# Block inverses of the gated delta stage: the transposes of five levels moved from TensorE to VectorE

## What is computed

```python
gam = jnp.exp(jnp.where(incl, dec[..., :, None] - dec[..., None, :], -jnp.inf))
a_low = jnp.where(strict, jnp.einsum('bhnid,bhnjd->bhnij', kb, k) * gam, 0.0)
t_inv = lax.linalg.triangular_solve(a_low + eye, jnp.broadcast_to(eye, a_low.shape),
                                    left_side=True, lower=True, unit_diagonal=True)
u = t_inv @ vb
w = t_inv @ (kb * jnp.exp(dec)[..., None])
```

## Time and profile before

| what | us |
|---|---|
| median of 3 runs | 2214.6 |
| lowest and highest run | 2213.84, 2214.62 |
| span of the profiled execution | 2213.1 |
| median less that span | 1.5 |
| TensorE busy in the span | 2182.9 (99%) |
| VectorE busy | 1497.0 (68%) |
| GpSimd busy | 1060.0 (48%) |
| ScalarE busy | 919.4 (42%) |
| L1466 (transposes), 192 in all | 27.9 |
| L1368 (masking), 96 in all | 33.8 |
| L1385 (copy_predicated), 96 in all | 42.8 |

### The profile page before, as it was taken

One profiled execution on the slowest core, in us unless ns is written; L12 is line 12 of the kernel. 1 busy time (PEld: TensorE's weight loads), 2 busy tenths in 40 slices (PEclk: granted clock), 3 DMA queues, 4 the chain that ended last, 5 costly groups with the idle time before them and its releaser, 6 DMA issues.

```text
span 2213.1 us, 29764 instructions
## 1 busy us (share of the span) xinstructions
PE 2182.9 (99%) x10592; PEld 1829.7 (83%) x10592; DVE 1497.0 (68%) x3595; ACT 919.4 (42%) x1514; POOL 1060.0 (48%) x850
## 2 busy tenths in 40 slices
PE   8999999999999999999999999999999999999998
PEld 6888888999888888888888888888888888888886
DVE  4655698777643530478888888972359788787883
ACT  6555596444433332433333333333323333333343
POOL 3433203544343344266666666656247665555500
PEclk9999999999999999999999999999999999999999
DMA  4222255552143322234444444456479999999940
GB/s 177 79 94 77 90 187 177 193 186 92 46 148 111 114 114 76 77 129 143 157 148 146 149 143 143 143 186 213 160 261 398 378 383 346 357 346 363 359 165 39
DMA packets 168831, 403.34 MB, mean 182 GB/s; under 512 B 27648, under 2 KB 101632, under 8 KB 158368
## 3 DMA queue, kind: packets, MB, share of 16 engines
q1 hardware_dynamic: 133920, 334.77, 43.3%
q0 software_dynamic: 34816, 67.41, 8.3%
HBM read 336.84 MB, written 65.28 MB: 182 GB/s over the span
## 4 chain that ended last, share of the span: by engine, by line
PE 71%; DVE 1%; ACT 1%; issue 0%; DVEq 0%; SPq 0%
PE ps L1628 13%; PE ps L176 11%; PE ps L174 11%; PE ps L175 11%; PE ps L2713 8%; PE ps L2714 8%; PE ps L2712 8%; PE ps L1971 1%; DVE down_v_low_sb L2535 0%; ACT merge_high_sb L1584 0%; PE ps L1718 0%; ACT ffn_norm_scaled_sb L1859 0%; DVE h_sb L1677 0%; DVE down_w_ple_proj_low_sb L2581 0%; DVE merge_low_sb L1589 0%
## 5 line engine op out<-in xcount | busy, mean ns | idle before, releaser
L2219 POOL DMA_INDIRECT g_dense<-up_gates_summed_sb,up_gate_at_sb x384 | 421.9, 1099 | 253.4 <-issue 211.7
L174 PE MATMUL ps<-n_high_sb,up_u_high_sb 128*128 128x512 f32 x1024 | 398.5, 389 | 0.5 <-issue 0.5
L176 PE MATMUL ps<-n_high_sb,up_u_low_sb 128*128 128x512 f32 x1024 | 398.5, 389 | 0.1
L175 PE MATMUL ps<-n_low_sb,up_u_high_sb 128*128 128x512 f32 x1024 | 398.3, 389 | 0.0
L2712 PE MATMUL ps<-down_v_high_sb,down_w_high_sb 128*128 128x512 f32 x768 | 298.8, 389 | 0.0
L2714 PE MATMUL ps<-down_v_high_sb,down_w_low_sb 128*128 128x512 f32 x768 | 298.8, 389 | 0.0
L2713 PE MATMUL ps<-down_v_low_sb,down_w_high_sb 128*128 128x512 f32 x768 | 298.8, 389 | 0.0
L2628 ACT ACTIVATE down_v_high_sb<-down_v_sb 128x1024 fp32r<-128x1024 f32 x120 | 125.8, 1048 | 310.8 <-PE ps L2714 286.9
L2062 DVE TENSOR_TENSOR up_u_low_sb<-up_u_sb,up_u_high_sb 128x1024 fp32r<-128x1024 f32 x128 | 156.3, 1223 | 140.1 <-ACT up_u_high_sb L2238 123.5
L2250 ACT ACTIVATE up_gelu_sb<-ps 128x512 f32<-128x512 f32 x128 | 76.5, 598 | 387.7 <-PE ps L176 280.7
L2444 POOL DMA_INDIRECT expert_rows_sb<-expert_v,chosen_expert_sb x128 | 155.1, 1212 | 168.6 <-DVE h_sb L2494 69.6
(11 more groups left out here) (382 smaller groups left out, 4484.0 us busy)
## 6 DMA issues: line engine op xcount, KB each, us to landing
up_u_sb<-expert_u SPq DMA_DIRECT2D x128, 512.0 KB
down_v_sb<-expert_v SPq DMA_DIRECT2D x32, 2048.0 KB
a_dense<-up_gelu_sb SPq DMA_DIRECT2D x128, 256.0 KB
g_dense<-nought_sb SPq DMA_DIRECT2D x8, 3072.0 KB, 12.0
down_gelu_sb<-a_dense SPq DMA_DIRECT2D x32, 768.0 KB
down_gates_sb<-g_dense SPq DMA_DIRECT2D x32, 768.0 KB
w_slots_sb<-w_conv SPq DMA_DIRECT2D x19, 1024.0 KB, 4.8
gate_w_sb<-w_gates SPq DMA_DIRECT2D x16, 512.0 KB, 4.4
```

The source lines that it names most:

```text
L174: pe.matmul(out, ah, bh, start=k == 0, stop=False)
L175: pe.matmul(out, ah, bl, start=False, stop=False)
L176: last = pe.matmul(out, al, bh, start=False, stop=k == n - 1)
L2219: pool.indirect_dma_start(cells, at, summed[:, tt, k:k + 1], None).then_inc(stored[tt], 16)
```

## The change

In the five levels with b up to 32 an inverse still has nothing outside its diagonal 32 by 32 squares, so a transpose of each square in its place is the transpose of the whole. VectorE now makes it with one instruction a lane (`dve.transpose`, 128x256, SBUF to SBUF) from `invs[u]` to `first_part[u]`, and then masks `first_part[u]` in place. First all four lanes are transposed, then all four masked. TensorE transposes only in the last level (b = 64); its wait for `inv_done` of each lane stays in every level. The semaphore `turned` now counts once a trip, and a new one, `squares_turned`, orders VectorE's masking behind its own transposes.

```diff
     NL = len(LEVELS)
+    SQUARE = 32
+    TURNS = sum(b <= SQUARE for b in LEVELS)
...
     split_done = [m.sem(f"gdn_inv_split{u}") for u in U]
+    squares_turned = m.sem("gdn_inv_squares_turned")
...
             for lv in range(NL):
-                for u in U:
-                    dve.wait_ge(turned, by_lane(u, i * NL + (lv + 1)))
-                    dve.tensor_tensor(first_part[u][:, :, :], both(whole4(u)), pair(halves[:, lv, :]), ALU.mult).then_inc(first_done, 1)
+                if LEVELS[lv] <= SQUARE:
+                    for u in U:
+                        dve.wait_ge(inv_done, by_lane(u, i * (NL + 1) + (lv + 1)))
+                        dve.transpose(first_part[u][:, :, :].rearrange("p c n -> p (c n)"),
+                                      invs[u][:, :, :].rearrange("p c n -> p (c n)")).then_inc(squares_turned, 1)
+                    for u in U:
+                        dve.wait_ge(squares_turned, by_lane(u, i * TURNS + (lv + 1)))
+                        dve.tensor_tensor(first_part[u][:, :, :], first_part[u][:, :, :], pair(halves[:, lv, :]),
+                                          ALU.mult).then_inc(first_done, 1)
+                else:
+                    for u in U:
+                        dve.wait_ge(turned, by_lane(u, i + 1))
+                        dve.tensor_tensor(first_part[u][:, :, :], both(whole4(u)), pair(halves[:, lv, :]), ALU.mult).then_inc(first_done, 1)
...
                     pe.wait_ge(inv_done, by_lane(u, i * (NL + 1) + (lv + 1)))
-                    for c in range(TS):
-                        last = pe.transpose(whole4(u)[:, c, :], invs[u][:, c, :], sq(m, "eye"))
-                    last.then_inc(turned, 1)
+                    if LEVELS[lv] > SQUARE:
+                        for c in range(TS):
+                            last = pe.transpose(whole4(u)[:, c, :], invs[u][:, c, :], sq(m, "eye"))
+                        last.then_inc(turned, 1)
                 if lv == 4:
                     second_gate(0, 11)
```

## The result

| | before | after |
|---|---|---|
| median of runs, us | 2214.61 (4 runs, 2213.84 to 2215.30) | 2252.86 (4 runs, 2251.53 to 2253.94) |
| ratio, 95% interval | | 1.0174, 1.0160 to 1.0188 |
| profiled execution, us | 2214.62 | 2251.53 |
| its span; mean granted clock | 2213.1; 0.999 | 2250.0; 0.992 |
| first matmul behind the stage's barrier starts at | 595.96 | 633.68 |

The kernel is 38.3 us slower. The time is inside the range (2235 to 2260), but 8 us above what my forecast case allowed for itself (2238 to 2245).

The account below looks back on a forecast made before the run. The prediction took a closed 4.68 us loop through VectorE's queue and TensorE as the bound. Its terms, 20.0 + 5.8 - 0.7 = 25.1 us, added to 2214.6 gave 2239.7 us; stated range 2235 to 2260.

Parts of the forecast that it names:

- my forecast case: Whole kernel: VectorE's four added transposes lengthen the loop, 25.1 us slower, 2239.7 us, own range 2238 to 2245; chance 0.70.
- The bound: a closed loop of 2.15 + 2.53: One doubling level: copy_predicated to first product 2.15, then to next copy_predicated 2.53, 4.68 us; TensorE's transposes fill its gap.
- What the change removes ... Worth: nothing.: TensorE: removing 160 of 192 transposes, eight in each of 20 levels, gains nothing apart from the fifth level.
- rival (d): TensorE's clock falls to half because it idles, doubling 3.67 us of passes in 17 levels: 62 us more, 2302; chance 0.03.
- The transpose's interval, 0.36: VectorE between fourth copy_predicated and first masking: one transpose issues every 0.36 us, four make 1.44 us.
- Rival (a): VectorE's transpose is dearer, an interval up to 0.61: 40.8 us more, 2255; chance 0.10.
- The masking meets GpSimd: the first product 3.69 after the CP: First masking, both inputs in SBUF, contends with GpSimd's second_part; first product 3.69 us after first copy_predicated, in place of 2.15.
- 1.54 a level: Lengthening from first copy_predicated to first product in 13 levels (second to fourth, last trip's fifth): 20.0 us.
- rival (b): VectorE's transpose, too, waits for GpSimd: 2.98 a level, 45.9 us more, 2260; chance 0.08.
- The first level, 1.44 each: First level of four trips: TensorE waits for VectorE, so four transposes add 1.44 each, 5.8 us.
- The fifth level, -0.7: Fifth level, first three trips: gate matmuls cover VectorE and no longer follow lane 3's transposes, gaining some 0.23 each.
- The delay passes the barrier whole: Barrier at the stage's end: it released TensorE and no transfer crosses it, so the whole delay reaches what follows.

Follow-up runs that it names:

- e4: Kernel before without TensorE's transposes in the second to fifth level, nothing added on VectorE, results not the reference's; 2216.51 us, ratio 1.0012.
- e2: Changed kernel with TensorE making the eight transposes in every level again, unused in the first five levels; 2240.25 us, ratio 1.0119.
- e1: Changed kernel with four unused 128x256 matmuls a lane on TensorE in the five levels, except where gate matmuls follow; 2241.47 us, ratio 1.0129.
- e3: Kernel before with VectorE's four transposes added in five levels, their results overwritten by the masking, which still reads PSUM; 2237.27 us, ratio 1.0107.
- e5: Changed kernel with VectorE's transposes and maskings of the next level placed between this level's copy_predicated, second to fifth level; 2256.87 us, ratio 1.0197.
- e10b: Changed kernel, transposes and maskings interleaved between copy_predicated, with TensorE's transposes made in every level, unused in the first five; 2242.02 us, ratio 1.0118.
- e7: Kernel before with lane 3 alone transposed by VectorE in the second to fifth level, order else as before; 2220.54 us, ratio 1.0029.

## Why the prediction was right in direction and 13 us short

1. *The bound: a closed loop of 2.15 + 2.53, with TensorE's transposes in its gap.* Right. e4 only takes transposes away, in 16 levels, and gains nothing.
2. *"What the change removes ... Worth: nothing."* **This step failed.** For the time on the path it held, but the transposes also kept TensorE's clock up. Without them eight levels run at half clock for 3.41 us each: 12.0 us by the trace, 12.6 us by e2, 11.4 us by e1. It is the mechanism of rival (d), to which I gave 0.03 and a wrong size: I priced it for all 17 levels at the full 32 passes (62 us), and it comes in 8, where it adds 1.5 each (12.0 / 8). What misled me was the earlier trace rows: a stretch of 5 us in another stage with 65% busy at 1.00, taken to speak for a level that idles 2.4 us at one piece. The rows could not carry that, and (d) at a fraction of the levels should have been a case with a real chance. Nor does the busy share decide: two levels of each trip of the change ran at 1.00 with TensorE busy for 60% (3.81 of 6.30).
3. *The transpose's interval, 0.36, between 0.33 and 0.447.* Right, measured 0.34 (0.335 in e3). Rival (a), 0.61, fell with it.
4. *The masking meets GpSimd: the first product 3.69 after the CP.* Right in mechanism. Measured 3.65 in e2 and 3.74 in the change. The forecast's 1.54 a level was 1.59: the masking ended 0.04 sooner than forecast (3.59, not 3.63), and the first product started 0.14 behind it, not the 0.055 of before, which I had not foreseen. By the Trainium skill's rule ("SBUF — State Buffer", "Who interferes with whom"), on which the prediction drew, the trace agrees: 0.599 for the masking with two SBUF inputs beside GpSimd, against its median of 0.412. The transposes themselves, at 401 to 439 ns, don't wait for GpSimd, so rival (b) fell too.
5. *The first level, 1.44 each.* Measured 1.3 to 1.4.
6. *The fifth level, -0.7.* **Wrong in sign**: +0.2. I took away lane 3's two transposes ahead of the gate matmuls, but those wait for lane 3's `inv_done` all the same, and with no transposes ahead of them they start only 0.35 after the last CP's end (393.69 + 1.79 = 395.48), 2.14 after the first CP in place of 2.04. e4, with the same program there, has 2.15. The cover by the gate matmuls held.
7. *The delay passes the barrier whole.* Right: 37.7 at the barrier, 38.3 in the median.

The terms other than the clock come to 26.4 us (20.7 + 5.5 + 0.2) where the forecast had 25.1. e1 and e2, with the clock held up, have 2241.5 and 2240.3, beside a forecast of 2239.7.

That 2252.9 still lies inside the stated range is luck. The range reached to 2260 for the sake of (a) and (b), a dearer transpose and a transpose that waits for GpSimd, and neither came; the 12 us that did come are of (d), which stood outside the range at 2302.

## What to carry to other kernels

Work in the waiting gap of an engine can be free, and then moving it away gains nothing, as in e4: ask first for the loop that closes around the gap, and then what stands ahead of the releasing instruction in its own in-order queue. Here that counted for more than how fast the moved operation is. Where a change makes TensorE idle for a large part of a short loop, price its clock as a case of its own, for a part of the repetitions, and check with an experiment that fills the gap with unused work. In this kernel a transfer of work between the two engines paid only together with an order that lets the relieved engine be the bound: one lane of four and a new order gained 0.2%, while either alone lost.

## What the runs showed of the hardware that I had not expected

- The granted clock is decided by more than the gap: in the change the same wait of 2.43 to 2.44 us stood before levels at 1.00 and before levels at half clock. It fell in the first and the fourth level of every trip, for 3.41 us each time. With transposes in the gap (e2, e3), or with a gap of 0.94 (e4), the traces show it at 1.00 in all four trips.
- The program doesn't decide it either. At the first level of the first trip the change and e5 have the same program and the same wait (2.63 and 2.64 us), and ran at 0.50 and 1.00; e10b and e2 have the same program and wait (1.18 and 1.19 us) there, and e10b fell to half while e2 didn't. What else decides which levels fall, the runs don't settle. So the 12 us are what this kernel paid in its four runs, and not a fixed price of such a gap.
- The first product comes 0.14 to 0.15 us behind the end of its masking where TensorE has no instruction between its wait for lane 3 and that product (the change, e4, e7), and 0.05 to 0.06 where it has one (before, e1, e2, e3). The length of the idle time before it doesn't sort these.
- VectorE's masking with two SBUF inputs took up to 0.93 us in place of 0.42 beside GpSimd (e5), while its transpose, with one, stayed at 0.40 to 0.44.
